# Prompt attention in pairs of heads with values stationary in column halves, row halves for two kinds of product, top-k rounds spread ahead

## The chip, the cores and the metric

The kernel runs on one core of a Trainium2 chip. The metric is the device time of one execution in microseconds (us). Before the change three executions took 1182.1, 1182.32 and 1185.39 us, with a median of 1182.32 us.

## The reference

The kernel computes one decoder layer for a prompt group (512 tokens, one sequence) and a sample group (8 sequences, one token each, with 2048 cached tokens). All data are float32. The parts that matter here are those on the prompt side:

```
# first group, 8 heads x 64: causal attention over 512 keys, query block of 128
s = (q_nope . k_nope + q_rope . k_rope) * MLA_SCALE;  p = exp(s - max);  o = (p @ v) / sum(p)

# second group, 8 query heads on 2 key/value heads (head h uses key/value head h // 4)
dots = einsum('bqhd,bkd->bqhk', q_idx, k_idx)              # 8 index heads x 64, one shared key
sc   = sum_h relu(dots_h) * w_idx_h                        # causal, -inf above the diagonal
_, sel = lax.top_k(sc, 128)                                # 128 of up to 512 keys per query
s = q . k_sel * DSA_SCALE + t5_bias;  p = softmax(s);  o = p @ v_sel
```

For the samples the kernel scores 2048 cached index keys per sequence, searches the threshold of their top 256, and attends to the cached latents and keys. After that come the output projection and a SwiGLU feed-forward part for all 520 tokens.

## The kernel before, in words

All order is written out by hand: each engine has a program of its own (`sp_program`, `pe_program`, `act_program`, `dve_program`, `pool_program`), and semaphores tie them together. TensorE writes into two PSUM tensors of two slots each: `psA` (counters `a_full`, `a_free`) and `psV` (`v_full`, `v_free`). A slot has two banks of 512 columns. The counters number all uses of slots in order, and use n may begin when use n-2 is free.

**Head and index stage.** The nine entries of `STEP` are the query tiles (five) and key tiles (four) of the first group. In step x TensorE makes the tile's projection (`head_up`, lines 800 and 804), then up to three index products (`index_product`, line 813), each for one (query block, index head) pair of `IQ`, and then turns the tile of step x-2 (`head_turn`, line 828). ScalarE squares (1431), takes roots (1438), does the `relu` of each index product into a ring `rb` of two (1450) and copies turned tiles back (1459). VectorE sums squares (1898), scales and rotates the tile (1910 to 1926) and adds each `relu` with its weight into the index scores `msk` (`weigh_index`, 1935). The index scores of query block 1, 2 and 3 have 256, 384 and 512 columns.

**Between the stages.** VectorE negates a small bias table (`g8`, line 1971). The SyncE queue writes it to memory and reads it back as a reversed table (`trev`, lines 540 and 543), and TensorE makes the bias matrix `toep` from it (854). Then follow small products for the samples, and the sample index pages: GpSimd fetches them by indirect DMA, two ahead, each fetch held until TensorE has turned the page two before (915), and TensorE multiplies them (905).

**Top-k rounds.** `top_rounds` finds 128 of each row's scores, 8 per round: a `max` (line 1960) and a `match_replace` (1961) on one block of `msk`. There are 16 rounds for each of the three query blocks, 48 in all. Before the change 22 stand ahead of the `relu` of the sample scores (2032), and the other 26 are spread over the attention by `ROUND_AT`. `search` is the threshold search of the samples, cut into short steps (2050 to 2071): 29 of them run in the attention (`half_steps`), the others in the decode stage. Every third step waits for a total from TensorE (`count_total`, 970).

**Prompt attention.** There are 64 units, one for each (group, query block, head) in `AT`. The first group goes through query blocks 3, 2, 1, 0 and the second through 0, 1, 2, 3, so the key width W is 512, 384, 256, 128 and then 128, 256, 384, 512. In turn u TensorE does three things: the scores of unit u+1 into `psV` (938), the transposes of the exponentials of unit u-1 into `psA` (949), and the products with values of unit u-2 (962). The last has the transposed exponentials (128x128 of a key block) as the stationary and the values (128x64) as the moving operand, so that the output lies by query in `psV`. VectorE adds the bias and takes the row minimum (2136), ScalarE takes the exponential with the row sum (1511) and copies the transposed block to SBUF (1518). After each eight units `take_group` divides by the sums (2119, 2122), and ScalarE's `square_mix` sums the squares (1499). For the second group GpSimd adds mask and bias ahead of VectorE (`combine`, 2474 and 2475): the first 11 results have buffers of their own, and the others use a ring of two, each held until VectorE has used the one two before.

**Decode stage.** 128 pages (`page`, `expand`), then sparse attention of the samples with the output projection, and the feed-forward part.

## Time and profile before

| quantity | value |
|---|---|
| median of three executions | 1182.32 us |
| profiled execution | 1180.58 us |
| its span, first to last instruction | 1178.8 us |
| mean granted TensorE clock | 0.987 of 2.4 GHz |
| TensorE busy | 1143.9 us, 97% of the span |
| VectorE busy | 681.6 us, 58% |
| ScalarE busy | 404.4 us, 34% |
| GpSimd busy | 101.3 us, 9% |

The profiled execution is 1.8 us longer than its span and 1.7 us below the median. PE is TensorE, PEld its weight load, DVE is VectorE, ACT is ScalarE, POOL is GpSimd and SPq the DMA queue of SyncE. A float32 matrix product has two records in the trace (two passes), a transpose has one. The time of one record runs from its issue to its modelled end, and records overlap; the distance between starts is what TensorE really needs for one.

### The profile page before, as it was taken

Reading aid. Unit: us, or ns where it says so; the run is one execution under the profiler, and the core shown is the slowest. Engines: PE = TensorE matmul, PEld = TensorE weight load, DVE = VectorE, ACT = ScalarE, POOL = GpSimd, SP = SyncE. Lnnn points to the kernel's source line nnn. Section 1 sums busy time; section 2 is a strip of 40 time slices with the busy share of each in tenths; the row PEclk is TensorE's granted clock in tenths of the full one; section 3 lists DMA queues with packets and bytes.
Section 4 is the critical chain, followed back from the end, with each engine's and each line's share of the span. In section 5 each row is a group of like instructions: output and inputs, shape, how many; then the busy total and the mean of one; then the engine's idle time right before and its main releaser. Section 6 shows DMA issues by size and latency. Waiting matters only on the chain.

```text
span 1178.8 us, 22158 instructions
## 1 busy us (share of the span) xinstructions
PE 1143.9 (97%) x9006; PEld 1008.9 (86%) x9006; DVE 681.6 (58%) x1533; ACT 404.4 (34%) x802; POOL 101.3 (9%) x155
## 2 busy tenths in 40 slices
PE   7999999998999999999999999999999999999998
PEld 5898986465587899999999877579999999999998
DVE  4545845735889787778886633464544545453440
ACT  4523224532477655555555423431101010100000
POOL 3100002001204500000000011100000000000000
PEclk9999999987999999999999999999999999999999
DMA  9996641022102202211124276623333333243340
GB/s 320 275 274 185 198 126 54 1 72 59 49 1 82 82 1 81 81 74 32 59 81 135 90 252 230 232 73 91 95 96 94 89 89 89 71 129 92 99 120 28
DMA packets 141875, 129.16 MB, mean 110 GB/s; under 512 B 17635, under 2 KB 135824, under 8 KB 139712
## 3 DMA queue, kind: packets, MB, share of 16 engines
q1 hardware_dynamic: 137184, 86.78, 25.2%
q0 software_dynamic: 4608, 41.23, 9.6%
q8 instruction: 58, 0.95, 0.3%
q14 instruction: 25, 0.20, 0.1%
HBM read 124.58 MB, written 3.41 MB: 109 GB/s over the span
## 4 chain that ended last, share of the span: by engine, by line
PE 81%; DVE 9%; ACT 4%; DMA 3%; issue 3%; SPq 0%; POOL 0%; ACTq 0%; DVEq 0%; POOLq 0%
PE psV L1254 21%; PE psV L1001 13%; PE psA L1254 11%; PE psA L669 8%; PE psV L1122 4%; PE psV L938 3%; PE psV L962 2%; PE psA L981 2%; PE psV L800 2%; DVE msk L1961 1%; PE psV L701 1%; PE psA L1051 1%; DVE top L1960 1%; PE psA L949 1%; PE psA L1087 1%
## 5 line engine op out<-in xcount | busy, mean ns | idle before, releaser
L1001 PE MATMUL psV<-r_r,wide_r 128*128 128x260 f32 x1536 | 207.5, 288 | 3.3 <-DVE msk L2194 2.9
L1001 PEld LDWEIGHTS psV<-r_r,wide_r 128*128 128x128 f32 x1536 | 190.4, 189 | 5.9 <-issue 3.3
L1552 ACT ACTIVATE wring<-psV 128x512 f32<-128x512 f32 x128 | 76.2, 597 | 91.4 <-PE psV L1001 69.0
L1254 PE MATMUL psV<-qiz_r,wring_r 128*128 128x260 f32 x528 | 93.9, 283 | 0.0
L2393 DVE TENSOR_TENSOR wide<-wide,psV 128x520 f32<-128x520 f32 x22 | 15.3, 696 | 125.0 <-PE psV L1254 125.0
L2195 DVE TENSOR_REDUCE msk<-wring 128x8 f32<-128x512 f32 x128 | 86.4, 676 | 0.0
L1254 PEld LDWEIGHTS psV<-qiz_r,wring_r 128*128 128x128 f32 x528 | 76.2, 188 | 0.0
L669 PE MATMUL psA<-wide_r,wring_r 128*128 128x260 f32 x416 | 76.1, 285 | 0.0
L1254 PE MATMUL psA<-qiz_r,wring_r 128*128 128x260 f32 x352 | 70.9, 283 | 0.0
L1254 PE MATMUL psA<-qiz_r,r_r 128*128 128x260 f32 x352 | 70.9, 282 | 0.0
L1254 PE MATMUL psA<-hT_r,r_r 128*128 128x260 f32 x352 | 70.8, 283 | 0.0
L2357 DVE TENSOR_TENSOR wring_r<-wring,r_r 128x1024 fp32r<-128x1024 f32 (+1 forms) x47 | 60.8, 1293 | 1.6
L669 PEld LDWEIGHTS psA<-wide_r,wring_r 128*128 128x128 f32 x416 | 60.7, 189 | 0.4
L2166 DVE TENSOR_TENSOR wide_r<-psA,wide_r 128x512 fp32r<-128x512 f32 x64 | 43.8, 684 | 24.1 <-ACT wide_r L1534 23.6
L1705 ACT ACT_TABLE_LOAD x11 | 14.1, 1283 | 117.2 <-PE psA L1254 117.2
L1254 PEld LDWEIGHTS psA<-qiz_r,r_r 128*128 128x128 f32 x352 | 54.3, 188 | 0.0
L1254 PEld LDWEIGHTS psA<-qiz_r,wring_r 128*128 128x128 f32 x352 | 54.3, 188 | 0.0
L1254 PEld LDWEIGHTS psA<-hT_r,r_r 128*128 128x128 f32 x352 | 54.1, 188 | 0.0
L1710 ACT ACTIVATE hT<-psA 128x512 f32<-128x512 f32 x8 | 4.8, 598 | 132.2 <-PE psA L1288 132.2
L1705 ACT ACTIVATE wide<-psA 128x520 f32 x22 | 13.3, 606 | 106.3 <-PE psA L1254 106.2
L2373 DVE SCALAR_TENSOR_TENSOR xT<-psV,modT,xT 128x260 f32 (+1 forms) x8 | 3.9, 488 | 76.6 <-PE psV L1254 76.6
L1534 ACT ACTIVATE wide_r<-psA 128x512 fp32r<-128x512 f32 x64 | 37.9, 593 | 17.5 <-PE psA L981 17.5
(565 smaller groups left out, 2576.4 us busy)
## 6 DMA issues: line engine op xcount, KB each, us to landing
wring<-w_ffn_in SPq DMA_DIRECT2D x44, 512.0 KB, 3.8
wide<-w_ada SPq DMA_DIRECT2D x11, 1024.0 KB, 6.6
wring<-w_ffn_out SPq DMA_DIRECT2D x16, 704.0 KB, 4.7
tok<-w_ada SPq DMA_DIRECT2D x9, 1024.0 KB, 5.4
wring<-w_in SPq DMA_DIRECT2D x24, 256.0 KB, 5.8
wring<-w_out SPq DMA_DIRECT2D x8, 512.0 KB, 6.6
wide<-w_out SPq DMA_DIRECT2D x2, 2048.0 KB, 8.1
r<-w_ada SPq DMA_DIRECT2D x3, 1024.0 KB, 10.7
```

The costliest lines, as they stand in the source:

```text
L669: mm = pe.matmul(sa(n)[:, hf, 0:HT], w[:, kk, :], x[:, kk, hf * HT:(hf + 1) * HT], start=(kk == 0 and w is high and x is hT_hi), stop=(kk ...
L800: mm = pe.matmul(out[0:w, c0:c1], qlatT[:, k, c:c + w], wuq[:, k, c0:c1], start=(k == 0), stop=(k == 2), skip_group_check=True)
L938: pe.matmul(sv(n)[:, 0, 0:W], lhs, rhs, start=True, stop=True).then_inc(v_full, 1)
L1001: mm = pe.matmul(kx[m % 2][:, hf, :], w, wtab[:, b % 2, l, 2 * k + hf, :], start=(k == 0 and w is high and l == 0), stop=(k == 1 and w is ...
L1122: mm = pe.matmul(psV[:, t % 2, 0, :], w, x[:, k, 0:SEQ], start=(k == 0 and w is high and x is xhigh), stop=(k == KD - 1 and w is low), ski ...
L1254: mm = pe.matmul(out[:, hf, 0:HT], w[:, k, :], x[:, hf * HT:(hf + 1) * HT], start=(k0 + k == 0 and x is xh and w is high), stop=(k0 + k == ...
L1534: nc.scalar.activation(lhi[p % 2], lps[p % 2], ACT.Identity).then_inc(lat_high, 1)
L1552: A(sq2[m % 2].rearrange("p (x n) -> p x n", x=2), kx[m % 2][:, :, 0:256], ACT.Square).then_inc(kx_squared, 1)
L1705: A(actT[:, bass.ds(i * 2 + s, 1), :].rearrange("p a (h t) -> p (a h) t", h=2), sa(A_G + s)[:, :, 0:HT], ACT.Silu).then_inc(a_free, 1)
L2166: v.tensor_tensor(llo[p % 2], lps[p % 2], lhi[p % 2].bitcast(F32), ALU.subtract).then_inc(lat_split, 1)
L2195: v.tensor_reduce(sums[b % 2][:, j, :], heads(sq2[m % 2]), AXX, ALU.add).then_inc(page_sums, 1)
L2357: v.tensor_tensor(low, raw, high.bitcast(F32), ALU.subtract).then_inc(w_split, 1)
```

## The change: what it does

1. Index products go in pairs: heads 2hp and 2hp+1 use rows 0 to 63 and rows 64 to 127 of the array and write into the two banks of one `psA` slot. One `relu` takes both. There are 12 products-in-pairs and 12 `relu`, one or two in a step (`index_at`), where there were 24 of each, three in a step. The 24 weighted additions on VectorE stay. The ring `rb` grows over part of `vm`, so ScalarE waits for all additions before it writes `vm`.
2. Attention goes in pairs of heads i and i+4 (`score_pair`, `turn_pair`, `value_pair`). In the second group the two score products lie in the row halves, and the pair waits until both `psV` slots are free. The transposes of both heads go to the two banks of one `psA` slot, of which there is now one, and one ScalarE copy takes both.
3. Values are the stationary operand (128x64, in column half e), and the transposed exponentials are the moving one (128 columns). The output lies by head dimension, head i+4e in PSUM rows 64e to 64e+63.
4. So each group of eight units needs a way back: VectorE copies the bank to SBUF (`copy_group`), TensorE turns it in four transposes (`turn_back`), and `take_group` divides from there. For the last group this lies in the first pages of the decode stage.
5. The rounds: 8 after `g8`, 15 after the samples' queries are prepared, 16 where there were 22, and 9 in the attention, in units 1, 3, ..., 19 (the tenth call there writes the last mask).
6. The 29 search steps of the attention are spread over units 16 to 56 in place of 51 to 63.
7. Several semaphores are merged, among them that of the last constant table (`far_loaded`), which the small bias product now waits for too.

```diff
-        IQ = [(qt, h) for qt in range(1, 4) for h in range(H)]
+        IQ = [(qt, hp) for qt in range(1, 4) for hp in range(H // 2)]
+        index_at = lambda x: range(3 * x // 2, 3 * (x + 1) // 2) if x < 8 else range(0)
-        AT = [(g, qt, h) for g, qt in GROUPS for h in range(H)]
+        AT = [(g, qt, h) for g, qt in GROUPS for h in (0, 4, 1, 5, 2, 6, 3, 7)]
-        half_steps = lambda u: 0 if u < 51 else 1 if u < 56 else 3
-        STEP_AT = [55 + k for k in range(9)]
+        COUNT_AT = [12 + 2 * k for k in range(KA)]
+        half_steps = lambda u: 0 if u % 2 or u < 16 or u > 24 + 4 * KA else 1 if u <= 24 or u % 4 == 0 else 2
...
             def index_product(j):
-                mm = pe.matmul(sa(n)[:, 0, 0:(qt + 1) * 128], qiz[:, h, qt * 128:(qt + 1) * 128],
-                               kidxT[:, 0:(qt + 1) * 128], start=True, stop=True)
+                for e in range(2):
+                    r = slice(64 * e, 64 * e + 64)
+                    mm = pe.matmul(sa(n)[:, e, 0:W], qiz[r, 2 * hp + e, qt * 128:W], kidxT[r, 0:W], start=True, stop=True)
...
+            def score_pair(p):
+                if g == 0:
+                    pair = [(qcat[0:QK, i + 4 * e, qs], kcat[0:QK, i + 4 * e, 0:W]) for e in range(2)]
+                else:
+                    pair = [(qz[64 * e:64 * e + 64, i + 4 * e, qs], kT[64 * e:64 * e + 64, 0:W]) for e in range(2)]
+                    pe.wait_ge(v_free, n)
+                for e, (lhs, rhs) in enumerate(pair):
+                    if g == 0:
+                        pe.wait_ge(v_free, n + e - 1)
+                    pe.matmul(sv(n + e)[:, 0, 0:W], lhs, rhs, start=True, stop=True).then_inc(v_full, 1)
+            def turn_pair(p):
+                pe.wait_ge(pt_taken, p)
+                for e in range(2):
+                    u = 2 * p + e
+                    pe.wait_ge(exp_done, u + 1)
+                    for kt in range(AT[u][1] + 1):
+                        mm = pe.transpose(psA[:, 0, e, kt * 128:(kt + 1) * 128], sP[:, u % 3, kt * 128:(kt + 1) * 128], ident)
+                    mm.then_inc(pt_full, 1)
+            def value_pair(p):
+                pe.wait_ge(pt_taken, p + 1)
+                if x >= 2 and p % 4 == 0:
+                    pe.wait_ge(o_copied, x - 1)
+                for kt in range(qt + 1):
+                    for e in range(2):
+                        mm = pe.matmul(psV[64 * e:64 * e + 64, x % 2, 1, i * 128:(i + 1) * 128], vv,
+                                       sPT[:, (2 * p + e) % 4, kt * 128:(kt + 1) * 128], start=(kt == 0), stop=(kt == qt), skip_group_check=True)
+                mm.then_inc(pv_done, 2)
...
+            for p in range(-1, NP + 1):
+                if p + 1 < NP:
+                    score_pair(p + 1)
+                if p == -1:
+                    sample_scores()
+                if p in COUNT_AT:
+                    count_total(pe, COUNT_AT.index(p)).then_inc(cnt_total, 1)
+                if p >= 6 and p % 4 == 2:
+                    turn_back(pe, p // 4 - 1)
+                if 0 <= p < NP:
+                    turn_pair(p)
...
+                if p >= 1:
+                    value_pair(p - 1)
...
+        def turn_back(pe, x):
+            pe.wait_ge(o_copied, x + 1)
+            pe.wait_ge(o_free, x)
+            for i in range(4):
+                mm = pe.transpose(o_by_pair(x)[:, i * 128:(i + 1) * 128], oS[x % 2][:, i * 128:(i + 1) * 128], ident)
+            mm.then_inc(o_turned, 1)
...
-                A(rb[:, j % 2, 0:W], sa(n)[:, 0, 0:W], ACT.Relu).then_inc(a_free, 1)
+                A(rb[:, j % 2, :, 0:W], sa(n)[:, :, 0:W], ACT.Relu).then_inc(a_free, 1)
...
+                if u >= 2 and u % 2 == 0:
+                    w = u - 2
+                    W = (AT[w][1] + 1) * 128
+                    act.wait_ge(pt_full, w + 2)
+                    if w >= 4:
+                        act.wait_ge(pv_done, w - 2)
+                    A(sPT[:, w % 4:w % 4 + 2, 0:W], psA[:, 0, :, 0:W], ACT.Identity).then_inc(pt_taken, 1)
...
-            EARLY = 22
-            ROUND_AT = list(range(8)) + [8, 10, 11, 13, 15] + [8 * x + y for x in range(2, 6) for y in (1, 4, 6)] + [48, 50]
+            ROUND_AT = list(range(1, 20, 2))
             v.tensor_scalar(g8, sv(V_BIAS)[0:8, 0, 0:384], -1.0, None, ALU.mult).then_inc(v_free, 1)
+            for _ in range(8):
+                next(rounds)
...
+            for _ in range(15):
+                next(rounds)
             v.wait_ge(v_full, V_KN + 1)
...
-            for _ in range(EARLY):
+            for _ in range(16):
                 next(rounds)
             v.wait_ge(v_full, V_IS + 1)
...
-                if u >= 8 and u % 8 == 3:
-                    take_group(u // 8 - 1)
+                if u >= 13 and u % 8 == 5:
+                    copy_group(u // 8 - 1)
+                if u >= 15 and u % 8 == 7:
+                    take_group(v, u // 8 - 1)
```

## Rows read from the trace of the kernel before

**Rows 1.** The page: an engine's busy time, and the chain's shares by engine.
```profile
PE 1143.9 (97%) x9006; PEld 1008.9 (86%) x9006; DVE 681.6 (58%) x1533; ACT 404.4 (34%) x802; POOL 101.3 (9%) x155
...
PE 81%; DVE 9%; ACT 4%; DMA 3%; issue 3%; SPq 0%; POOL 0%; ACTq 0%; DVEq 0%; POOLq 0%
```

**Rows 2.** Stretches: length, busy PE, PEld, DVE, ACT, POOL; clock, DMA share, GB/s.
```profile
185.00:242.00 57.00, 52.95 (x203) 28.43 (x202) 40.34 (x86) 29.02 (x61) 5.56 (x11) 1.00 0.08 23
242.00:308.50 66.50, 59.52 (x235) 37.11 (x234) 35.11 (x106) 18.15 (x30) 8.74 (x11) 0.82 0.27 80
308.50:325.30 16.80, 16.76 (x95) 12.23 (x96) 13.74 (x39) 8.97 (x21) 3.97 (x9) 0.90 0.00 1
325.30:339.20 13.90, 13.90 (x97) 11.37 (x97) 11.25 (x35) 9.19 (x26) 0.00 (x0) 1.00 0.01 2
339.20:364.10 24.90, 22.34 (x162) 19.58 (x162) 22.40 (x82) 19.54 (x78) 1.19 (x1) 1.00 0.24 89
364.10:386.20 22.10, 21.58 (x139) 17.06 (x139) 20.04 (x62) 16.24 (x56) 15.37 (x23) 1.00 0.02 9
386.20:404.50 18.30, 18.30 (x123) 14.28 (x122) 15.44 (x57) 11.24 (x27) 12.15 (x16) 1.00 0.01 2
```

**Rows 3.** The chain that ended last, index stage: start, length, what.
```profile
204.68 3.89 PE psV L800 x12
...
212.48 3.98 PE psV L800 x12
```

**Rows 4.** Groups by form, 185 to 242 us: busy us, mean ns, idle before.
```profile
L1935 DVE SCALAR_TENSOR_TENSOR msk<-r,wtok,msk 128x384 f32<-128x384 f32 x7 | 4.3, 608 | 0.2
...
L1450 ACT ACTIVATE r<-psA 128x384 f32<-128x384 f32 x8 | 3.6, 478 | 0.1
L828 PEld LDWEIGHTS psA<-mats,wring 128*64 128x64 f32 x32 | 3.4, 111 | 2.4 <-ACT wide L1459 1.3 <-ACT r L1450 0.6 <-issue 0.6
```

**Rows 5.** Timeline of DVE between the stages: start, length, what, idle before.
```profile
251.50 1.23 DVE L1975 COPY wring<-psV 128x1024 f32<-128x1024 f32 x1 [8.59 <-PE psV L854]
...
277.07 0.68 DVE L1996 COPY rope<-psV 8x512 f32<-8x512 f32 x1 [18.57 <-PE psV L887]
...
307.08 1.22 DVE L2032 TENSOR_SCALAR r<-psV 128x1024 f32<-128x1024 f32 x1
```

**Rows 6.** The chain that ended last, one unit of width 512 in the attention.
```profile
316.58 0.91 PE psV L938 x2
317.49 0.44 PE psA L949 x4
317.93 0.84 PE psV L962 x8
```

**Rows 7.** Timeline of PE in the decode stage: products in quarter columns.
```profile
453.82 1.93 PE L1051 MATMUL psA<-wide,r 128*32 128x256 f32 x32
455.57 0.59 PE L1051 MATMUL psA<-tok,r 128*32 128x256 f32 x2
456.09 0.66 PE L981 MATMUL psA<-mats,wide 128*128 128x128 f32 x4
```

**Rows 8.** Groups by form, 310 to 412 us, the attention.
```profile
L1961 DVE MATCH_REPLACE8 msk<-top,msk 128x512 f32<-128x512 f32 x16 | 10.8, 675 | 0.0
L1511 ACT ACTIVATE r<-r,stat 128x512 f32<-128x512 f32 x15 | 10.8, 719 | 8.4 <-DVE stat L2136 8.3
...
L1518 ACT ACTIVATE r<-psA 128x512 f32<-128x512 f32 x16 | 9.4, 590 | 6.7 <-PE psA L949 6.7
...
L2136 DVE CUSTOM_DVE_ANT_0 r<-psV,wring 128x512 f32<-128x512 f32 x8 | 5.4, 680 | 0.0
...
L1518 ACT ACTIVATE r<-psA 128x128 f32<-128x128 f32 x16 | 4.3, 266 | 0.1
```

**Rows 9.** Timeline of POOL, one unit of width 512.
```profile
392.24 0.63 POOL L2475 TENSOR_TENSOR wring<-msk,wring 128x256 f32<-128x256 f32 x1
393.21 0.95 POOL L2474 TENSOR_SCALAR wring<-msk,wring 128x256 f32<-128x256 f32 x1 [0.34 <-DVE stat L2136]
```

More of the change, by code:

```diff
@@ L213, in build @@
         for x in range(len(STEP)):
-            A_IQ += [nA + y for y in range(3 if x < 8 else 0)]
-            nA += 3 if x < 8 else 0
+            A_IQ += [nA + y for y in range(len(index_at(x)))]
+            nA += len(index_at(x))
             if x >= 2:
@@ L311, in build @@
         kx = [psV[:, x, :, 0:260] for x in range(2)]
-        lps = [psA[:, (A_PT + x) % 2, 0, :] for x in range(2)]
+        lps = [psA[:, x, 0, :] for x in range(2)]
+        o_by_pair = lambda x: psA[:, 1, 0, :] if x < 7 else psA[:, 0, 1, :]
+        oS = [hT[:].rearrange("p a t -> p (a t)")[:, 1024 + x * 512:1536 + x * 512] for x in range(2)]
         krps, ropeps, latp = psA[:, 0, 1, :], psA[:, 1, 1, 0:128], psA[:, 1, 1, 0:256]
@@ L833, in pe_program @@
                     head_up(x)
-                for j in range(3 * x, min(3 * x + 3, 24)):
+                for j in index_at(x):
                     index_product(j)
@@ L1464, in act_program @@
                     squares(x)
-                    if x < 8:
-                        relu(3 * x)
+                    for j in index_at(x)[0:1]:
+                        relu(j)
                     head_roots(x)
-                    for j in range(3 * x + 1, min(3 * x + 3, 24)):
+                    for j in index_at(x)[1:]:
                         relu(j)
@@ L1606, in act_decode @@
                 square(m)
+                if m == 1:
+                    square_mix(act, 7)
+                if m == 2:
+                    act.wait_ge(o_squared, 8)
+                    A(ss8, ss8, ACT.Sqrt, scale=1.0 / 512, bias=epsc[:]).then_inc(mix_root, 1)
                 if j == 1:
```

183 lines of the change are left out of this document (80 added, 103 removed).

## The prediction

> **What bounds the kernel now.** I read the page first, then the stretches, then the chain of waits with a timeline of the places that the change touches. The page has TensorE busy for 97% of the span and carrying 81% of the chain that ends last [rows 1]. So what counts is time taken off TensorE's own line of work, and waits of TensorE. The change touches three stretches. In the index stage (185 to 242 us) TensorE is marked busy for 52.95 of 57 us, but VectorE for 40.34 [rows 2]. The chain there shows a rhythm: a projection of 3.9 us starts every 7.8 us [rows 3]. The other 3.9 us are index products, a turn of 1.1 us, and waits for the third `relu`. Between the stages (242 to 308.5 us) VectorE stands idle twice, for 8.59 and 18.57 us, and then works on top-k rounds until 307.08 us, when the sample scores are taken and the attention can begin [rows 5]. The attention itself (308.5 to 404.5 us, five stretches) is not one thing: with widths 512 and 384 in the first group TensorE is busy throughout (16.76 of 16.80 and 13.90 of 13.90 us); with small widths VectorE is at 22.40 of 24.90 us and ScalarE at 19.54; at the end TensorE again at 18.30 of 18.30 [rows 2].
>
> **Index stage.** TensorE: 24 products become 12 pairs. ScalarE: two `relu` of 0.48 us at width 384 become one of some 0.81 (an estimate: the slope between the copies of 128 and 512 columns, 0.266 and 0.590 us, is 0.84 ns a column [rows 8], so 384 more columns cost 0.32). VectorE keeps its 24 additions. I follow the steps. A step with one pair needs 3.9 us of projection, 0.8 of product and 1.1 of turn, and the turn no longer waits for a `relu`, because only one slot is used before it: 5.8 us. A step with two pairs has its turn wait for the first `relu`: 3.9 + 0.8 + 0.9 + 1.1 = 6.7 us. The mean of 6.25 stands against 7.8. But now VectorE binds: of its 40.34 busy us [rows 2] none goes, and it can only start when the first projection (3.9 us) and its squares are done, 5.3 us into the stretch. It has three weighted additions a step, 0.61 us each at width 384 [rows 4], and I find it at work nearly without a gap from step 1 on. 190.3 us plus 40.3 plus some 4 us of gaps gives 234.6 against 242: **7 us saved**. If row halves do not overlap, TensorE's steps are longer by 0.7 to 1.4 us, and 4 us are left. Bounds: 2 and 9.
>
> **Between the stages.** The first 8 rounds (query block 1) take 2 x (0.42 + 0.07) = 0.98 us each, 7.8 us, in a gap of 8.59. The next 15 (8 of width 256, 7 of width 384 at 1.25) take 16.9 with the mask, in a gap of 18.57 [rows 5]. Both are covered, with 0.7 and 1.6 us to spare; without that cover each us over would be on the path. The last batch is 9 x 1.25 + 7 x 1.5 = 21.7 us where 22 rounds took 23.5, so it is done 1.8 us sooner. Nothing is gained by that: what is late next is the page fetches and products on TensorE, which finish at 306.8. Their queue moves whole with the start of the stage, because the first fetch waits on VectorE after `g8` and each later one on TensorE. So the 7 us are passed on, and the stretch keeps its 66.5 us. The merged waits name loads that land some 50 us before they are needed: nothing. The granted clock in this stretch has a mean of 0.82 [rows 2]; nothing in the change fills it.
>
> **Attention, the unit costs.** Now one unit of width 512 is 0.91 of scores, 0.44 of transposes, 0.84 of values, 2.19 us [rows 6]; narrower ones are in proportion (0.70, 0.49, 0.27 for scores; 0.11 and 0.21 for each key block of the others).
> - Values: no row shows a 64-column half. The nearest is the 17 products with quarter columns: one of 256 columns has 1,024 column passes, 0.427 us, so five in one quarter need 2.13 us. From 453.82 to the next transposes at 456.09 are 2.27 [rows 7]. So quarters do run side by side, weight loads included, for 0.14 us around them. I take the same for halves: a key block of a pair costs 0.213 us where it was 0.42. Bounds: 0.213 (all overlapped) and 0.87 (loads of 0.111 [rows 4] and passes of 0.107 one after another, four of each).
> - Scores in row halves: no row at all. I take full overlap and 0.15 us for the change of shape, 0.91 + 0.15 for a pair of 1.82. Bounds: 0.91 and 1.82 + 0.3.
> - So TensorE per pair of width 512, 384, 256, 128: first group 3.70, 2.85, 2.0, 1.1; second 2.95, 2.3, 1.65, 1.0 us.
> - ScalarE per pair: two exponentials (0.82 with the read of the sum at 512) and one copy (0.16 + 0.84 ns a column): 2.66, 2.23, 1.79, 1.35 us [rows 8].
> - VectorE per pair: 2 x 0.62 at width 512, down to 2 x 0.21; a round 1.5 (0.675 for each half, and the load of values [rows 8]); three search steps 1.25. New are the copies, 0.65 each, eight of them; the take costs the same 0.84. The turns back add 0.44 us of TensorE each, and a wait: they stand right behind the scores, while the copy is still under way, about 1 us where TensorE binds.
> - GpSimd in the ring: 0.95 + 0.63 = 1.6 us for each unit of width 512 [rows 9], hidden under 2.2 now, 3.2 a pair afterwards: more than TensorE's 2.95.
>
> The trace agrees only in part with what the Trainium skill has on tiles. "TensorEngine Tiling (Array Packing)", Key Properties, says that a change of tiling mode drains the engine; rows 7 show 0.14 us for it, which is in the sum above.
>
> **Attention, by stretch.**
> - First group, 512: four pairs at 3.70 are 14.8 for eight units at 2.19, 17.5: 2.7 less. VectorE's 11 us (four rounds) are hidden.
> - First group, 384: TensorE 11.4, VectorE 3.9 + 6 + 1.5 = 11.4, and the wait before the turn back, together 12.3 against 13.9: 1.6 less.
> - Units 16 to 39, 24.9 us now [rows 2]. The rounds leave (10 of the old 12), but the search steps and copies come. Width 256: VectorE 2.8 + 3.4 (two rounds, the mask) + 1.5 + 3.2 (first four steps) = 10.9. The two eights of width 128: ScalarE 4 x 1.35 + 0.7 = 6.1 each, and in the second group a pair waits for both slots (score 0.27 and hand-over 0.2, then 0.21 + 0.6 + 0.21 + 0.1 on VectorE = 1.6), so 6.5 and 6.8. Sum 24.2: 0.7 less.
> - Units 40 to 55, 22.1 us now: at width 256 score 0.49 + 0.2, additions and steps 0.35 + 0.65 + 0.35 + 0.1 = 2.15 a pair, 9.0 with the turn back. At 384, 2.6 a pair, 11.0; the tables hide under the scores. Sum 20.0: 2.1 less.
> - Second group, 512: 8 x 2.2 = 17.6 now, then GpSimd's 4 x 3.2 = 12.8: 4.8 less.
> - The join: of the old 6 us from the last scores to the first page, the reciprocal and squares leave the path, but a pair's exponentials and its copy of 1024 columns come: nothing. The last turn back costs 0.4.
>
> That is 11.9 less 0.4, **11.5 us**. With the index stage 18.5 us come off the profiled execution of 1180.6 (span 1178.8 and 1.8 around it): 1162.1. That execution was 1.7 below the median, so I expect **1164 us**. Decode and feed-forward parts have the same instructions, but for a square root moved by two pages.
>
> **The rivals.**
> - *Everything overlaps better.* Each stretch of attention then costs only its busiest engine: 14.8, 11.4, 10.9, 6.1, 6.1, 7.9, 9.9, 12.8, in all 79.9 us against some 96: 16 less; the index stage gives 9; 25 in all: **1157**. For it: TensorE does run at 13.90 of 13.90 now [rows 2]. Against: pairs share one transpose buffer and, in the second group, both score slots. Chance 20%.
> - *Halves do not overlap.* The kernel before shows only quarters. A pair then needs 4 x 0.427 for values and 1.82 for scores; TensorE's load is 70 + 17 + 10 = 97 us, what it was. What is left is the index stage (4) and the stalls of small widths (3): **1175**. The same time comes if the pairs' lock-step eats what TensorE gives. Chance 15%.
> - *Loads stand between the halves: slower.* Each value product waits for its own load: 0.87 us for a key block of a pair, against 0.213 in the sum. Over 80 of them that is 52 us on TensorE, so attention ends 40 us later than forecast: **1204**. It decides from 0.45 us on, where the 18.5 us are used up. For it: no trace shows the load of a half beside a product in the other. Against: rows 7. Chance 6%.
> - *The change does not do what it says in the index stage:* VectorE or the fetches absorb it, and only attention gives: **1171**. Against: the rounds before the attention are done first [rows 5]. Chance 9%.
>
> On the third, the Trainium skill ("TensorE: Matmul & The Clock Gate", Part 3, The mechanism) says that weight loads overlap products in flight only when the row group differs. Here both halves have the same row group, so by that rule the loads would not be hidden; against it speaks the pace of 0.84 us for eight full loads and products in one row group [rows 6].
>
> **How the numbers follow.** Forecast 50%: 1160 to 1168. Better overlap 20%, no overlap 15%, slower 6%, index absorbed 9%. The range from 1149 to 1176 leaves out the slow case and the tails. No change means within 0.3% (3.5 us), about what a measurement can tell here. Slower takes the 6% and a tail of the lock-step case, together 8%; the same gets 4%; faster 88%.
>
> **What would show it.** The small bias product should fall from 241 to near 234 us, with VectorE idle under 5 us in the steps. VectorE should reach the end of its 8 and 15 rounds before TensorE is ready. Value records of 128 columns should start 0.05 to 0.06 us apart in the mean, four to a key block. In the last eight units GpSimd should have no idle time. The forecast is wrong if the records of the two halves start one behind the other, if attention with narrow widths becomes longer than now, or if the 7 us come back before 308 us.

## The result, and the profile after

Four executions of the changed kernel took 1163.57 to 1167.05 us, median 1165.11; the kernel before took 1182.1 to 1185.39 beside them, median 1183.19. The ratio is 0.984 (95% interval 0.982 to 0.986), 18.1 us less. The forecast was 1164. The profiled execution took 1163.57 us with a span of 1161.8.

Two lines of the page after, against [rows 1]: busy time, and the chain's shares. TensorE lost 18.8 us of marked busy time and is as full as before, 97%.

```profile
PE 1125.1 (97%) x9038; PEld 983.1 (85%) x9038; DVE 686.5 (59%) x1541; ACT 398.9 (34%) x758; POOL 101.6 (9%) x155
...
PE 85%; DVE 7%; ACT 3%; issue 2%; DMA 2%; POOL 0%; ACTq 0%; DVEq 0%; POOLq 0%
```

The stretches after, cut where those of [rows 2] are, with the same columns. The index stage is full on VectorE (40.06 of 50 us, where it was 40.34 of 57). With narrow widths (328.6 to 374) no engine is full any more.

```profile
185.00:235.00 50.00, 46.81 (x203) 24.03 (x201) 40.06 (x86) 27.26 (x49) 5.54 (x11) 0.98 0.08 27
235.00:300.00 65.00, 58.64 (x236) 36.40 (x234) 55.86 (x156) 17.99 (x30) 7.96 (x8) 0.83 0.26 81
300.00:315.60 15.60, 15.07 (x88) 9.49 (x86) 12.08 (x31) 8.34 (x17) 4.76 (x11) 0.89 0.01 2
315.60:328.60 13.00, 13.00 (x106) 9.14 (x102) 10.55 (x30) 8.61 (x21) 0.00 (x0) 1.00 0.00 1
328.60:352.00 23.40, 22.08 (x186) 16.39 (x184) 19.66 (x93) 18.40 (x67) 1.19 (x1) 1.00 0.27 101
352.00:374.00 22.00, 17.93 (x152) 11.29 (x148) 18.03 (x61) 15.67 (x45) 15.69 (x23) 1.00 0.01 4
374.00:391.60 17.60, 16.84 (x158) 11.20 (x154) 8.56 (x25) 13.42 (x31) 12.23 (x17) 1.00 0.26 96
```

The chain of waits in the index stage after, to be held against [rows 3] (start, length, what). The projections start 5.7 and 6.7 us apart, where it was 7.8.

```profile
195.06 4.07 PE psV L804 x12
...
200.77 3.87 PE psV L804 x12
...
207.47 3.98 PE psV L804 x12
```

The timeline of VectorE between the stages, against [rows 5]. The idle time of 8.59 us is down to 2.40, and the sample scores wait 1.25 us for TensorE's product: the first 8 rounds and the last 16 are covered. Between them the 15 rounds end at 270.09 us, and VectorE's next copy, which waited 18.57 us before, starts at 270.15 us without a wait.

```profile
246.54 1.23 DVE L2015 COPY wring<-psV 128x1024 f32<-128x1024 f32 x1 [2.40 <-PE psV L859]
...
299.83 1.22 DVE L2074 TENSOR_SCALAR r<-psV 128x1024 f32<-128x1024 f32 x1 [1.25 <-PE psV L909]
```

The chain for one pair of width 512 in the second group, against two of [rows 6]. Scores of two heads, transposes of two, values of two take 3.10 us where two single heads took 4.38. The 16 value records (two for each product) start 1.02 / 16 = 0.064 us apart.

```profile
380.30 1.06 PE psV L946 x4
381.36 1.02 PE psA L955 x8
382.38 1.02 PE psV L969 x16
```

To compare kernels I cut each trace at the same events: the first projection of the head, the small bias product, the taking of the sample scores, VectorE's first addition of each width, and the first page. All are lengths in us; the columns 512 to 512 are the eight units of each width, first group and then second, and the last one ends with the first product of the first page. Behind the stroke is the granted clock of a stretch of attention where it is below 1.00.

| kernel | head starts | index | between | 512 | 384 | 256 | 128 | 256 | 384 | 512 | attention |
|---|---|---|---|---|---|---|---|---|---|---|---|
| before | 185.2 | 56.3 | 65.6 | 17.77/.90 | 14.32 | 9.23 | 15.25 | 8.91 | 13.52 | 21.20 | 101.5 |
| after | 185.2 | 49.1 | 65.5 | 15.55/.89 | 13.02 | 8.86 | 14.21 | 10.17 | 12.25 | 16.45 | 91.8 |
| idx_full_rows | 190.7 | 51.1 | 63.7 | as after | | | | | | | 91.8 |
| idx_single | 190.8 | 56.3 | 68.1 | 13.86 | 13.02 | 8.86 | 14.21 | 10.17 | 12.24 | 16.45 | 90.1 |
| scores_full_rows | 185.4 | 49.2 | 65.8 | 15.56/.89 | 13.01 | 8.86 | 14.26 | 10.42 | 12.69 | 18.66 | 94.8 |
| halves_in_turn | 190.3 | 49.0 | 65.8 | 16.52/.90 | 14.14 | 9.73 | 14.23 | 10.18 | 12.51 | 17.95 | 96.6 |
| values_moving | 188.2 | 48.4 | 67.1 | 15.00 | 14.06 | 9.60 | 16.34/.78 | 14.66/.50 | 12.66/.92 | 18.45 | 102.1 |
| values_moving_2 | 185.1 | 49.2 | 66.5 | 18.35/.81 | 14.05 | 9.60 | 16.90/.73 | 14.66/.50 | 16.23/.68 | 18.44 | 109.6 |
| own_slot_wait | 188.4 | 48.4 | 66.1 | 13.87 | 13.02 | 8.86 | 13.96 | 9.55 | 12.23 | 16.45 | 89.3 |
| rounds_back | 187.9 | 48.4 | 65.8 | 15.09 | 12.96 | 11.51 | 22.10/.64 | 13.63/.70 | 14.47/.88 | 16.45 | 107.5 |
| before_rounds | 189.3 | 56.3 | 65.4 | 16.15 | 14.26 | 8.93 | 12.55 | 8.11 | 12.89 | 21.29 | 95.5 |
| steps_late | 190.2 | 49.1 | 65.7 | 15.56/.89 | 13.01 | 8.86 | 14.20 | 8.10 | 11.69 | 18.23 | 91.0 |
| own_slot_steps_late | 191.1 | 48.9 | 66.0 | 15.55/.89 | 13.02 | 8.86 | 13.94 | 8.11 | 11.67 | 18.52 | 91.0 |
| short_search | 188.6 | 48.4 | 65.7 | 13.87 | 13.01 | 8.87 | 14.20 | 8.11 | 11.68 | 17.33 | 88.4 |

Two columns differ between executions of any kernel. The head starts between 185.1 and 191 us, with a granted clock of 0.97 down to 0.86 in the first 60 us; and the first 512 stretch has a clock of 0.89 or of 1.00, which is 1.68 us (15.55 against 13.87 for the same instructions). The index stage of the changed kernel is 49.1 us at a clock of 0.98 and 48.4 at 1.00. Single times of one kernel so differ by several us for nothing (thirteen executions of the kernel before, beside experiments 4 to 7, took 1178.57 to 1190.14 us), and the stages decide.

One row hides a loss: the second group's 256 stretch went from 8.91 to 10.17 us, longer than before the change, and its 384 stretch from 13.52 to 12.25.

### The profile page after: what moved, and what is told of

It is laid out like the page before. It is cut to its first block, busy times and chain, and to the rows that moved or that the text cites. A ratio compares the mean times of both kernels' runs of the same rounds, so it can differ in the third digit from the quotient of the medians.

```text
span 1161.8 us, 22104 instructions
## 1 busy us (share of the span) xinstructions
PE 1125.1 (97%) x9038; PEld 983.1 (85%) x9038; DVE 686.5 (59%) x1541; ACT 398.9 (34%) x758; POOL 101.6 (9%) x155
## 4 chain that ended last, share of the span: by engine, by line
PE 85%; DVE 7%; ACT 3%; issue 2%; DMA 2%; POOL 0%; ACTq 0%; DVEq 0%; POOLq 0%
PE psV L1290 22%; PE psV L1033 15%; PE psA L1290 11%; PE psA L673 9%; PE psV L1158 4%; PE psV L946 3%; PE psA L1013 2%; PE psV L705 2%; PE psV L804 2%; PE psA L1083 2%; PE psV L969 1%; PE psA L955 1%; DMA r<-cache_idx,rows_of 1%; PE psV L714 1%; PE psA L1123 1%
## 5 line engine op out<-in xcount | busy, mean ns | idle before, releaser
L1568 ACT ACTIVATE wide_r<-psA 128x512 fp32r<-128x512 f32 x64 | 37.9, 593 | 18.0 <-PE psA L1013 17.8
```

Of the source, the lines that this page charges most:

```text
L1568: nc.scalar.activation(lhi[p % 2], lps[p % 2], ACT.Identity).then_inc(lat_high, 1)
```

## The experiments

**1. Index products over full rows** (idx_full_rows). The pairs stay, but each product uses all 128 rows.

```diff
-  pe.matmul(sa(n)[:, e, 0:W], qiz[r, 2 * hp + e, qt * 128:W], kidxT[r, 0:W], ...)
+  pe.matmul(sa(n)[:, e, 0:W], qiz[:, 2 * hp + e, qt * 128:W], kidxT[:, 0:W], ...)
```

> The changed kernel with its index products over all 128 rows (the other head's rows are zero), two per slot and one relu as now. Read at the small bias product, which ran at 241.45 us before and 234.37 after the change. Theory A, VectorE and the slot order set the pace: TensorE's 7.7 us of extra product time (half of 15.3) mostly hides, the bias product comes at 235 to 237 us. Theory B, the row halves give the gain: it comes at 239 to 242 us. The rest of the kernel keeps its lengths.

The index stage took 51.1 us, 2.0 longer than in the changed kernel and 2.7 longer than its 48.4 at the same clock of 1.00, so the halves do save TensorE time. Counted from the changed kernel's start, the bias product would come at 236.2 us, as theory A has it. But the stretch behind it was 1.8 us shorter (63.7), at a granted clock of 0.87 in place of 0.83. So the sample scores were taken 114.7 us after the head's start, and in the changed kernel too. Time 1169.15 us, of which 5.5 are the later start. The row halves of the index products were worth nothing at the end. That is one execution, and the clock made up for the loss; what it would be worth at an equal clock was not measured.

**2. Index products one by one** (idx_single), as before, with all else changed.

```diff
-  IQ = [(qt, hp) for qt in range(1, 4) for hp in range(H // 2)]
+  IQ = [(qt, h) for qt in range(1, 4) for h in range(H)]
   ...   (three products in a step, each over all rows, one per slot)
-  A(rb[:, j % 2, :, 0:W], sa(n)[:, :, 0:W], ACT.Relu).then_inc(a_free, 1)
+  A(rb[:, j % 2, 0, 0:W], sa(n)[:, 0, 0:W], ACT.Relu).then_inc(a_free, 1)
```

> The changed kernel with the old index stage: 24 products over all rows, one per slot, 24 relus, three in a step. Both theories: bias product at 241 to 242 us, 7 us later than after the change, and the whole kernel 7 us longer (span 1168 to 1169), if the 7 us are passed on to the end. A rival: the page fetches or the last batch of rounds absorb it, and the attention begins less than 4 us later than after the change.

The stage was back at 56.3 us: all of the 7.1 us hang on the pairs, and the rival (something behind the stage absorbs them) is out. The time was 1177.78 us, with a span 14.2 us above that of the changed kernel, more than the 7 that were expected: 5.6 are the later start, 7.1 the stage, 2.5 the stretch behind it (68.1 us at a clock of 0.80), less 1.7 in attention's first stretch with its full clock; the rest lies behind the first page. Waits of this kernel in the index stage (engine and line, what it waits for: us in all, times, longest): VectorE stands for the squares of each tile, and TensorE's turn (L831) and products (L817) for a `relu`.

```profile
DVE wring L1933 <- ACT wring L1465: 16.2, 7, 8.2
...
PEld psA L831 <- ACT r L1484: 5.9, 6, 1.3
PEld psA L817 <- ACT r L1484: 5.2, 8, 0.8
```

The longest of VectorE's 16.2 us, 8.2, is the wait for the first tile, at the stage's start, which every kernel has; 8.0 are left. In the changed kernel, from 191 us on and so without that first wait, VectorE's same wait is this, and with the 0.4 us of another it is all its idle time up to the bias table:

```profile
DVE wring L1935 <- ACT wring L1467: 1.5, 2, 1.0
```

**3. Scores of the second group over full rows** (scores_full_rows).

```diff
-  pair = [(qz[64 * e:64 * e + 64, i + 4 * e, qs], kT[64 * e:64 * e + 64, 0:W]) for e in range(2)]
+  pair = [(qz[:, i + 4 * e, qs], kT[:, 0:W]) for e in range(2)]
```

> The second group's scores over all 128 rows again, in pairs, with the same wait for both slots. Theory A, the pair stands in lock-step with VectorE, so each microsecond of scores is on the path in the whole second group: four pairs each of 0.12, 0.34, 0.55 and 0.76 us more, 7 us in all, spread over units 32 to 63. Theory B, VectorE or GpSimd bind there: less than 3 us.

Attention was 2.95 us longer (1167.62 us), just inside theory B's 3 and far from theory A's 7: 2.2 of it in the last eight units, 0.4 at 384, 0.25 at 256, nothing at 128. My reading is that at narrow widths the second product of a pair lies behind VectorE's first addition, so that most of TensorE's longer time shows only at 512.

**4. The column halves one after the other** (halves_in_turn), not alternating.

```diff
-  for kt in range(qt + 1):
-      for e in range(2):
+  for e in range(2):
+      for kt in range(qt + 1):
```

> The changed kernel with the loops of value_pair exchanged: all key blocks of head i in the lower column half, then all of head i+4 in the upper. Theory A, the queue of TensorE is in order and a half waits for itself: the halves overlap only at the seam, value records of a pair of width 512 need 1.5 to 1.8 us in place of 1.0, and the attention is 4 to 8 us longer. Theory B, the engine takes products of the other half from further back: no difference.

Attention was 4.8 us longer (1174.77 us, start 5.2 us late), as theory A has it, and the 16 value records of a pair of width 512 took 1.51 us on the chain (from 391.25 us on) in place of 1.02. Groups of value products by form (busy us, mean ns of one), this kernel, then the changed one: one record lasts 283 ns in both, but together they fill more time. That fits an engine that takes them in order, so that two halves meet only at the seam.

```profile
L969 PE MATMUL psV<-r 128*64 128x128 f32 x160 | 15.3, 283 | 0.0
```
```profile
L969 PE MATMUL psV<-r 128*64 128x128 f32 x160 | 12.3, 283 | 0.0
```

**5. Values as the moving operand** (values_moving, values_moving_2), as before the change, in pairs. Then there is no turn back. The first form lets the two heads' sums alternate within one bank over all its rows and so does not compute the reference's result; its time stands only for that order of work:

```diff
-  mm = pe.matmul(psV[64 * e:64 * e + 64, x % 2, 1, i * 128:(i + 1) * 128], vv, sPT[...], ...)
+  mm = pe.matmul(psV[:, x % 2, 1, h * 64:(h + 1) * 64], sPT[...], vv, ...)
```

> Pairs as now, but the values are the moving operand (64 columns) again and the exponentials the stationary one: no column halves, no copy, no turn back. Theory A: column halves shorten only the stretches where TensorE binds, so without them the first group at 512 and 384 is 2 to 3 and 1 to 2 us longer, the last eight units 2 to 3 us, and the middle (units 16 to 55) is shorter by up to 2 us because VectorE has no copies: the kernel 3 to 6 us longer. Theory B: the 17 us of TensorE time count nearly whole: 12 us or more longer.

It took 1177.5 us, attention 102.1, 10.3 more than with the change; its clock was 0.78 at 128, 0.50 at the second 256 and 0.92 at the second 384. The second form computes head after head:

> As values_moving (no column halves, no copy, no turn back), with the key blocks of one head finished before the other head begins, since interleaved heads share one bank. Its stages are read from the first row minimum of each width to the next, since the granted clock of the start differs from run to run. Theory A: column halves are worth 3 to 6 us of the attention (91.8 us from the sample scores to the first page with them). Theory B, from the look at values_moving, where the granted clock fell in the second group: half of the worth is the clock, and the stretch is 97 to 102 us again with a clock under 0.95. If the clock stays at 1.0, 93 to 97 us.

Median 1179.86 us (1169.47 to 1185.51; ratio to before 0.995, 0.992 to 0.999). Attention took 109.6 us, 17.8 more and above both ranges. Where the clock was 1.00, the price is TensorE's: 1.03 at 384, 0.74 at 256, 1.99 in the last eight, and from the first form 1.13 at 512 (15.00 against 13.87). Together that is 4.9 us, within theory A's 3 to 6. In the other stretches the clock was lower, and price and clock can't be told apart there. The ten executions bear this out: two, with a mean granted clock of 0.983 and 0.980, took 1169.47 and 1170.63 us, and the other eight, with 0.965 to 0.972, took 1176.52 to 1185.51. So of the 14.8 us by medians I put some 5 down to the column halves, and the rest came with a lower clock. Stretches of the second form (columns as in [rows 2]):

```profile
333.00:343.00 10.00, 10.00 (x77) 9.39 (x77) 8.08 (x31) 7.12 (x21) 0.00 (x0) 1.00 0.00 1
343.00:359.70 16.70, 15.39 (x107) 13.85 (x105) 10.52 (x60) 12.17 (x48) 1.19 (x1) 0.77 0.38 143
359.70:374.40 14.70, 14.47 (x61) 11.21 (x62) 6.94 (x28) 7.48 (x24) 5.63 (x9) 0.50 0.01 1
```

**6. Each head waits for its own score slot** (own_slot_wait) in the second group too.

```diff
-      pe.wait_ge(v_free, n)
   for e, (lhs, rhs) in enumerate(pair):
-      if g == 0:
-          pe.wait_ge(v_free, n + e - 1)
+      pe.wait_ge(v_free, n + e - 1)
```

> In the second group each score product waits only for its own psV slot, as in the first group, not for both. Theory A: the wait for both puts the scores on VectorE's path in each pair (VectorE waits 11.7 us for scores, TensorE 5.9 for row minima), so without it units 32 to 63 are 3 to 5 us shorter. Theory B: the pair then starts one by one, the row halves no longer overlap, and the loss cancels the gain: within 1 us.

The second group was 0.9 us shorter (0.25 at 128, 0.62 at 256, nothing else), where theory A had 3 to 5: theory B's number. Its reason is seen once, at 256, where the two score products of a pair start at 354.53 and 355.46 us; what that costs was not measured. Median 1163.59 (ratio 0.984, 0.979 to 0.989), no difference from the changed kernel that can be told.

**7. The rounds back** (rounds_back) where they were: 22 ahead of the sample scores, 26 up to unit 50.

```diff
-  ROUND_AT = list(range(1, 20, 2))
+  ROUND_AT = list(range(8)) + [8, 10, 11, 13, 15] + [8 * x + y for x in range(2, 6) for y in (1, 4, 6)] + [48, 50]
   (no rounds after g8 and after the samples' queries, 22 in place of 16 before the sample scores)
```

> The changed kernel with the rounds where they were: 22 ahead of the sample scores, 26 in the attention. Theory A, VectorE would bind the pairs: its load of 69 us in the attention rises by 17 rounds of 1.25 to 1.5 us, so the attention is 10 to 16 us longer than 91.8, most of it in the widths 256 and 128; the sample scores are taken at the same time or up to 1 us earlier. Theory B, the rounds fit between the pairs: less than 5 us longer.

1182.42 us: attention 107.5, longer than before the change and 15.7 longer than with it, in theory A's range. At full clock the loss is 1.2 us in the first stretch and 2.65 at 256; then VectorE binds, TensorE has idle time between its pairs, and the clock falls too, so the 15.7 are not the rounds' alone. Below are two stretches of this kernel, and TensorE's waits for VectorE's additions from 330 to 378 us (us in all, times, longest):

```profile
330.00:341.70 11.70, 10.70 (x88) 7.71 (x84) 10.78 (x36) 7.91 (x23) 0.00 (x0) 1.00 0.00 1
341.70:363.80 22.10, 18.38 (x104) 12.12 (x104) 19.71 (x80) 11.60 (x44) 1.19 (x1) 0.67 0.29 108
```
```profile
PEld psV L946 <- DVE stat L2170: 11.9, 16, 2.0
PE psV L946 <- DVE stat L2170: 6.9, 8, 1.6
```

**8. The rounds alone** (before_rounds), in the kernel before.

```diff
-  ROUND_AT = list(range(8)) + [8, 10, 11, 13, 15] + ... + [48, 50]
+  ROUND_AT = list(range(1, 20, 2))
   (8 rounds after g8, 15 before knew, 16 before the sample scores, as in the change)
```

> The kernel before with one part of the change alone: 8 rounds after the small bias table, 15 after the samples' queries, 16 ahead of the sample scores and 9 in units 1, 3, ... 19 in place of 26 spread to unit 50. Heads stay single, the search steps stay in units 51 to 63. Theory A (the rounds are a condition, not a source): with TensorE busy throughout at widths 512 and 384 nothing is to be had there; only the narrow widths lose VectorE work (12 rounds of about 1.5 us in units 16 to 50, of which TensorE and ScalarE cover most), so the attention goes from 101.5 us to 97 to 100. Theory B (the rounds moved ahead are half of the attention's gain or more): 96 or less. The index stage stays at 56 us and the stretch between the stages at 65.5 in both.

1178.94 us against a median of 1185.03 beside it. Attention took 95.5 us, 6.0 less. Of that 1.62 are in the first stretch, which had the full clock here and 0.90 before; if I put them down to the clock, 4.4 us are the rounds': 2.70 at 128, 0.80 and 0.63 at 256 and 384 of the second group, 0.30 at 256. Theory B's bound (96) was met by the raw number, and nearly half of the gain of 9.7 is what it said; theory A holds only for the wide stretches of the first group (384: 14.26 against 14.32). From 339 to 361 us VectorE was now at 13.64 of 22.00 us, where it had 22.40 of 24.90 [rows 2].

```profile
339.00:361.00 22.00, 21.50 (x168) 19.93 (x167) 13.64 (x58) 19.28 (x75) 1.19 (x1) 1.00 0.09 23
```

**9. The search steps of units 40 to 55 moved to the last eight units** (steps_late).

```diff
-  half_steps = lambda u: 0 if u % 2 or u < 16 or u > 24 + 4 * KA else 1 if u <= 24 or u % 4 == 0 else 2
+  half_steps = lambda u: {56: 1, 58: 3, 60: 3, 62: 3, 63: 3}.get(u, 0) if u >= 40 else (as above)
   (and COUNT_AT, TensorE's totals for them, moved along)
```

> The changed kernel with the 12 search steps of units 40 to 55 (and the last one) moved into units 56 to 63. Asked is why units 40 to 55 took 22.4 us, as before, where 20.0 were forecast. Theory A (VectorE's search steps stand between its additions, and GpSimd's work beside them makes them longer): the two stretches fall from 10.17 and 12.25 us to at most 9.2 and 11.2, 2 us or more in all; the last eight units get at most as much longer. Theory B (the hand-over from pair to pair binds: two slots, two exponentials, one transposed block): they stay within 0.7 us of 22.4, and the last eight are 1 to 3 us longer than 16.45.

Units 40 to 55 took 19.79 us, 2.6 less than 22.42, and the last eight 18.23, 1.8 more. Theory B is out, and theory A holds but for its 11.2 at 384 (8.10 and 11.69 were measured). That 19.79 is near the 20.0 of the prediction says nothing: the prediction had the steps in its 20.0. Twelve steps have 5.6 us of VectorE's marked time in 22, and 4.5 at the means that they have where GpSimd is nearly idle. Groups of the changed kernel by form, first 328 to 352 us, where GpSimd is nearly idle, then 352 to 374 us, where its `combine` works:

```profile
L2106 DVE TENSOR_TENSOR wring<-wring 128x136 f32<-128x136 f32 x4 | 1.2, 300 | 0.1
L2107 DVE TENSOR_REDUCE wring<-wring 128x8 f32<-128x136 f32 x4 | 1.2, 295 | 0.1
L2113 DVE TENSOR_TENSOR wring<-wring 128x8 f32<-128x8 f32 x4 | 0.7, 166 | 0.1
...
L2106 DVE TENSOR_TENSOR wring<-wring 128x136 f32<-128x136 f32 x4 | 2.0, 501 | 0.1
L2107 DVE TENSOR_REDUCE wring<-wring 128x8 f32<-128x136 f32 x4 | 1.2, 295 | 0.1
L2113 DVE TENSOR_TENSOR wring<-wring 128x8 f32<-128x8 f32 x4 | 1.1, 282 | 0.1
```

The four L2106 of the second window took 0.30, 0.75, 0.31 and 0.64 us. The 0.75 starts 0.04 us behind an addition of GpSimd (L2526) and outlasts it, and VectorE's second addition of that pair comes 1.55 us behind its first, where a pair without steps has 0.35:

```profile
357.53 0.42 DVE L2174 CUSTOM_DVE_ANT_0 r<-psV,wring 128x256 f32<-128x256 f32 x1 [0.79 <-PE psV L946]
...
358.08 0.75 DVE L2106 TENSOR_TENSOR wring<-wring 128x136 f32<-128x136 f32 x1
358.87 0.29 DVE L2107 TENSOR_REDUCE wring<-wring 128x8 f32<-128x136 f32 x1
359.08 0.41 DVE L2174 CUSTOM_DVE_ANT_0 r<-psV,wring 128x256 f32<-128x256 f32 x1
```
```profile
358.04 0.64 POOL L2526 TENSOR_TENSOR wring<-msk,wring 128x256 f32<-128x256 f32 x1 [0.58 <-DVE stat L2174]
```

With both, own slots and late steps (own_slot_steps_late):

> The same, and each head of the second group waits for its own score slot alone, as in the first group. If both theories hold a part, units 40 to 55 take 20.0 to 20.8 us here, against 22.4 in the changed kernel, 21.8 with the own slots alone; attention from the sample scores to the first page 87.5 to 89 us. If the hand-over alone binds, 21.5 or more, and the whole is no faster than with the own slots alone (1163.6).

Units 40 to 55 took 19.78 us, the last eight 18.52; attention 91.0, median 1166.98 (1164.39 to 1169.78, ratio 0.984, 0.982 to 0.988). Without the steps the own slots give nothing there (8.11 and 11.67 against 8.10 and 11.69): my reading is that the two were one wait, the second addition of a pair held back by a step. The expected 87.5 to 89 was missed, also if 1.7 us are taken off for the clock of 0.89 in the first stretch: the last eight units have no room for 13 steps, although VectorE is busy there for only half of the time (8.56 of 17.60 us in the changed kernel). My reading, not tested by itself, is that each step holds back an addition for which GpSimd's ring waits.

**10. A shorter search in the attention** (short_search): nine steps go to the decode stage, four to units 56 and 58.

```diff
-  KA = 8
+  KA = 5
+  half_steps = lambda u: {56: 1, 58: 3}.get(u, 0) if u >= 40 else (as above)
   (and COUNT_AT to match)
```

> The changed kernel with 9 of the 29 search steps of the attention moved into the decode stage's pages (the search then ends 12 pages later, at page 114 in place of 102), the 4 that are left of units 40 to 55 moved to units 56 and 58. Theory A (the steps beside GpSimd's work cost what they take, and where VectorE has idle time they are free): units 40 to 55 take 19.8 us, as with all steps moved to the end, the last eight 16.4 to 17.0, so attention is 89 to 89.6 us at the same clock in its first stretch (91.8 in the changed kernel), and the decode stage keeps its length, since VectorE is busy there for about half of the time: 2.2 to 2.8 us less in all, 1161 to 1163 by the median. Theory B (a later search holds up the sequences' masks, or the pages): the decode stage ends 2 us or more later, and the median stays at 1164 or above.

Units 40 to 55 took 19.79 us, the last eight 17.33; attention 88.4 at full clock in the first stretch, against 90.1 for that of the changed kernel at full clock: 1.7 us less, where 2.2 to 2.8 were expected; the last eight units missed their 16.4 to 17.0. The decode stage began 0.5 us earlier than in the changed kernel, was 0.5 us longer, and both spans are 1161.8. Median 1165.25 (1160.52 to 1166.03, six executions; ratio 0.984, 0.981 to 0.986), not theory A's 1161 to 1163. The median is in theory B's range, but the decode stage's 2 us or more are not there. So no version beat the changed kernel by what can be measured.

## Why the prediction was right, step by step

| term | forecast | measured |
|---|---|---|
| index stage | 7 | 7.1 |
| between the stages | 0 | 0.1 |
| first group 512 | 2.7 | 2.2 |
| first group 384 | 1.6 | 1.3 |
| units 16 to 39 | 0.7 | 1.4 |
| units 40 to 55 | 2.1 | 0.0 |
| last eight, join, turn back | 4.4 | 4.7 |
| sum | 18.5 | 16.9 |

- *Index stage.* Right in size and mechanism. VectorE's 40 us set it, and it had 1.9 us of idle time in the steps where "under 5" was written. Experiment 2 gives the whole 7.1 to the pairs, experiment 1 nothing in the end to their row halves, so the bound for "row halves do not overlap" (4 us left) had the mechanism of the first 2 us but not that they came back behind it. The small bias product came at 234.3 us, as forecast.
- *Between the stages.* The 7 us were passed on. The spare times are not those worked out, and TensorE's clock is in them. The first 8 rounds had 2.40 us to spare where 0.7 was forecast, since TensorE's products there ran at 0.50 of the clock from 234.3 to 238.3 us, where it was 1.00 before; with the clock at 1.00 (experiment 1) VectorE waited 0.93 us. The 15 rounds had nothing to spare where 1.6 was forecast: from the first product with the reversed table to those that VectorE waits for, TensorE took 21.9 us, and 24.0 before (its clock was 0.75 in most of it, where it had been 0.60). They ended just in time, so the sign "before TensorE is ready" did not hold for them, though they cost next to nothing.
- *Values in column halves.* 0.213 us a key block and 0.15 for the change of shape make 1.00 us for a pair of width 512; the chain has 1.02. So halves overlap in full, weight loads included, though both use all rows. The third rival (loads between the halves, 1204) is out. The rule that the prediction cites beside it from the Trainium skill ("TensorE: Matmul & The Clock Gate", Part 3, The mechanism) says that a weight load overlaps products in flight only when the row group differs; the trace does not agree here, with 0.064 us for a record and its load. The same section also lets loads into a background weight buffer go ahead, and with that the pace is no contradiction. Experiment 4 shows what the overlap needs: neighbours in the instruction stream in different halves.
- *Scores in row halves.* Forecast 0.91 + 0.15 = 1.06, chain 1.06. Experiment 3 prices it at 2.95 us over the second group.
- *GpSimd in the last eight units.* Forecast 3.2 us a pair against TensorE's 2.95, and no idle time. Measured, 374 to 391 us: 0.94 + 0.64 us a unit, 3.15 a pair, and half a microsecond idle. But TensorE's pair took 3.10 (transposes 1.02 where 0.88 was taken), and the chain runs through TensorE from 379.49 to 384.51 us. The two are level; that GpSimd alone sets the pace is not shown.

```profile
L2525 POOL TENSOR_SCALAR wring<-msk,wring 128x256 f32<-128x256 f32 x7 | 6.6, 939 | 0.5 <-DVE stat L2174 0.4
L2526 POOL TENSOR_TENSOR wring<-msk,wring 128x256 f32<-128x256 f32 x8 | 5.1, 637 | 0.0
```

- *Units 40 to 55: the step that failed.* "at width 256 score 0.49 + 0.2, additions and steps 0.35 + 0.65 + 0.35 + 0.1 = 2.15 a pair, 9.0 with the turn back. At 384, 2.6 a pair, 11.0; the tables hide under the scores." Measured were 10.17 and 12.25, 2.4 us more than 20.0, and nothing was saved where 2.1 were forecast. The starts of VectorE's additions tell where (the forecast's 2.6 at 384 split in the same form):

| from, to | width | forecast, us | measured in four pairs, us |
|---|---|---|---|
| first addition to second | 256 | 1.00 | 1.09, 1.20, 1.55, 0.76 |
| second to next pair | 256 | 1.15 | 1.22, 1.22, 1.21, 1.92 |
| first addition to second | 384 | 1.13 | 1.24, 0.99, 1.55, 0.90 |
| second to next pair | 384 | 1.47 | 1.56, 2.02, 1.56, 2.43 |

Between the two additions of a pair 0.8 us in all were too much. That is the search steps, taken at the price they had alone; beside GpSimd one of their operations takes up to 0.75 us in place of 0.30 (experiment 9). From the second addition to the next pair 1.7 us were too much, after 1.0 for the turn back is allowed. Of that 0.46 is the second table, which did not hide: it takes 1.62 us where it took 1.22, and the next addition, 2.02 us behind the last, starts as it ends. Some 0.7 are in the last pair of each width, where TensorE has the turn back and the first, wider scores of the next width; the rest is spread over the hand-overs.

So the steps' price is a third of the miss. That moving them away gave 2.6 us (experiment 9) is another matter: by the forecast's own 0.65 a pair it would have given 5.2, but the rest of the path, longer than forecast, held the stretch at 19.8.

```profile
367.24 1.62 DVE L2202 TENSOR_TENSOR r_r<-wukv,r_r 128x1024 fp32r<-128x1024 f32 x1
368.78 0.54 DVE L2174 CUSTOM_DVE_ANT_0 r<-psV,wring 128x384 f32<-128x384 f32 x1
```

- *A sign that came true.* The prediction called itself wrong if attention with narrow widths became longer than now. Over all three narrow stretches it did not (33.2 us against 33.4), but at 256 in the second group it did, 10.17 against 8.91.
- *Units 16 to 39* came out better by 0.7, so the total held: in part luck, since the misses have different causes. The parts did not work as written: the rounds alone give 3.0 us there in single heads (experiment 8), and pairs with search steps then take 1.6 back (21.48 to 23.07 us). Own slots explain 0.25 of it; whether the steps or the pairs' hand-over take the rest was not tried.
- *What the pairs are worth by themselves,* from experiment 8 to experiment 10, both at full clock: 2.3 + 1.2 + 0.1 - 1.6 + 0 + 1.2 + 3.9 = 7.1 us (with the search steps moved as well), all of it at widths 512 and 384. The rounds are worth 4.4, and the pairs cannot be had without them (experiment 7).

The spans fell by 17.0 us (1178.8 to 1161.8), all of it before the first page: behind it both kernels take 770 us. The 1.5 us that are missing from 18.5 are the failed 2.1 and 0.8 of the first group, made up in part by units 16 to 39 and the last eight. The medians fell by 18.1, since the profiled execution of the kernel before was 2.6 us below its median and that of the changed kernel 1.5; that is within what executions of one kernel differ by.

## What to carry to other kernels

Column halves overlapped only between neighbouring instructions here, so alternate them, and count 0.15 us for each change of shape (for row halves the order was not tried). Work put into an engine's idle time is not free if it stands between two instructions that another engine waits for, and an operation of VectorE with two SBUF inputs took up to 0.75 us in place of 0.30 beside GpSimd. Before you make TensorE faster, move the other engines' work out of the stretch: here the same pairs lost all their gain in attention when VectorE still had its rounds, part of it with the clock. When you explain a miss, go by the starts of the instructions on the path: moving a piece of work away and finding the forecast time can be chance.

## What was unexpected of the hardware

- *TensorE's clock.* In experiments 5 (both forms) and 7 the granted clock fell from 1.00 to 0.50 (2.4 to 1.2 GHz) in the middle of attention. In experiment 7 TensorE had waited on VectorE with more than a quarter of the stretch 338 to 342 us idle, and again from 348 on; in experiment 5 it had been marked busy for 1.65, 1.58 and 1.46 of each 2 us before the fall at 352 us. But the changed kernel has shares just as low (1.42, 1.50 and 1.75 of 2 us from 346 on) and kept 1.00. So TensorE had idle time before these falls, but such idle time was not always followed by one, and what decides was not found. The two shortest of the second form's ten executions (experiment 5) speak for a fall that does not come in each.
- *VectorE and GpSimd slow each other.* From 352 to 374 us GpSimd's half of 128 columns takes 0.80 us in the mean (first row), and 0.65 in experiment 8 from 361 to 382 us (second row), where VectorE was busy for 13.05 of 21 us in place of 18.03 of 22.

```profile
L2525 POOL TENSOR_SCALAR wring<-msk,wring 128x128 f32<-128x128 f32 x8 | 6.4, 800 | 1.0 <-DVE stat L2174 1.0
```
```profile
L2477 POOL TENSOR_SCALAR wring<-msk,wring 128x128 f32<-128x128 f32 x8 | 5.2, 652 | 2.9 <-DVE stat L2139 2.8
```

One beside the second table (367.24 to 368.86 us, shown above) took 1.57 us where the one before it took 0.60:

```profile
366.57 0.60 POOL L2525 TENSOR_SCALAR wring<-msk,wring 128x128 f32<-128x128 f32 x1
...
367.75 1.57 POOL L2525 TENSOR_SCALAR wring<-msk,wring 128x128 f32<-128x128 f32 x1
```

The reduce (L2107) did not slow in experiment 9's rows, though two of its four, at 364.00 and 370.12 us, ran beside a GpSimd instruction; the operations with two SBUF inputs (L2106, L2113) did, when they began just behind a GpSimd addition. That is what the Trainium skill says ("SBUF — State Buffer", Who interferes with whom): a VectorE instruction with two SBUF inputs contends with a GpSimd instruction that reads SBUF, a reduce never does. The trace agrees, with means of 0.50 against 0.30 us for L2106 and 0.295 us in both windows for the reduce.

- *The start.* The same instructions before the head took 185.1 to 191 us, with 0.97 to 0.86 of the clock in the first 60 us. A comparison by single executions would have drowned most of these experiments.
